# A two-layer decoder block pair in fp32: turned up-projections grouped by width, a second gate bank, sums of squares behind the last blocks, and a token factor moved to the output

## The chip, the cores and the metric

The kernel runs on one core of a Trainium2 chip. The metric is the device time of one launch in microseconds. TensorE is called PE in profile rows, its weight loads PEld, VectorE DVE, ScalarE ACT, GpSimd POOL and the queue of DMAs SP.

## What is computed

The input is one sequence of 256 tokens with 1024 features. A first network of two layers is followed by a second one of two layers. Cut to what the change touches:

```
first network, each layer:
    h = rms_norm(x, norm_mix);  proj = h @ w_in          # queries, keys, values, 2048 gate logits
    y_a = dilated_attention(...) @ w_proj_a
    y_b = stick_breaking_attention(...) @ w_proj_b
    gates = sigmoid(gate_logits + b_gate)
    x = x + (gates[:1024] * y_a + gates[1024:] * y_b) @ w_out
    h = rms_norm(x, norm_ffn)
    up = h @ w_up;  a, b = up[:2816], up[2816:]
    a = causal_conv(a, 3 taps) + conv_b
    x = x + (silu(a) * b) @ w_down
x = rms_norm(x, norm_final)
second network, each layer:
    x = x + rms_norm(mixer(rms_norm(x)));  x = x + rms_norm(cross_attention(rms_norm(x), mem))
    x = x + rms_norm(square(relu(rms_norm(x) @ w1)) @ w2)     # w1: 1024 x 4096
```

All matmuls are computed to nearly fp32 accuracy from operands split into a high and a low part: x @ w = xhi whi + xhi wlo + xlo whi.

## The kernel before

**Weights.** SP brings every weight matrix in chunks of 1 MB (2048 columns for each of 128 partitions) into three slots `raw`. Each chunk has two halves; ScalarE casts a half to `whi` (line 1416) and VectorE subtracts it to `wlo` (line 1799), into four slots; TensorE takes halves in one fixed order and waits on `lo_done`. All engines run through orders that are written out by hand, so where an engine waits, everything behind it on that engine waits too.

**Streams.** Ahead of a projection, `x` is turned on TensorE (line 960) in four blocks of 256 features. ScalarE writes the high part, scaled by the norm's gain (lines 1441 and 1442), and VectorE the low part (line 1826, two instructions a block, `stream_lo`). The first chunk behind a stream waits for block after block. The norm's factor per token, `rstd`, isn't in the stream: `squares` (line 1849, VectorE, two instructions of 1024 features) makes the sums, POOL the root (`root`, line 720), and the factor is applied to products later.

**Turned chunks** (`turned_half`, lines 870 to 891). The up-projections of the first network and w1 of the second yield feature rows instead of token rows: the weights are the stationary operand, the activations the moving one. For a block of 128 features (f = 0, 1) and each of 8 slices k of the inputs there is a wide matmul (line 888: `whi` times high and low part side by side, 512 columns) and a narrow one (line 889: `wlo` times the high part, 256 columns). So a chunk has 16 pairs, in two halves. There are 22 up blocks (11 in each layer) of two chunks each (a and b) and 32 chunks of w1 (16 in each layer). The first chunk behind a stream (four in all) is issued with that stream.

**Up-projection pipeline.** For each block: ScalarE copies the part that belongs to the low activations out of PSUM (lines 1582 and 1590), VectorE adds the other (lines 2111 and 2116), POOL multiplies a by the row of token factors (line 763), VectorE convolves (lines 2126 and 2132), ScalarE applies SiLU into `sl` (line 1604), POOL multiplies this by the row again into `gated` (line 768), VectorE multiplies by b (line 2146), and high and low part (lines 1610 and 2153) go into w_down, two blocks later. The row is made once for each layer: `spread_row`, two transposes on TensorE (line 902), and a copy by ScalarE (line 1498). At the end VectorE adds the product to x (line 2181).

**MLP pipeline.** ScalarE copies (1758), VectorE adds (2492), takes relu and multiplies by the row (2497), squares (2501), ScalarE makes the high part (1764) and VectorE the low one (2505). `spread_row` stands between w1(0) and w1(1) on TensorE.

**Gates.** The 2048 gate logits come in eight chunks of 256 columns, all accumulated in PSUM bank 7, both token tiles side by side. TensorE issues their halves between the steps of the attentions (`gate_half`): halves 2, 3 and 4 (chunk 1 and the first half of chunk 2) in a row, then the sums of the stick-breaking part, which wait for the four `keep` tiles of VectorE (line 2026); half 8 (chunk 4) stands behind the first scores of the dilated attention. VectorE evicts a chunk with the token factor and the bias (`gate_out`, line 1991, two instructions). Before chunk c starts, TensorE waits until chunk c-1 is out:

```
if h == 0 and c:
    pe.wait_ge(gate_pre, 2 * (NGC * l + c))
half_chunk(plan.jobs["gate", l, c][0], h, ahi, alo, 0, [[(0, GC, 7)], [(0, GC, 7)]], True, True, None, (0, GC))
```

## Time and profile before

| | |
|---|---|
| median of 3 runs | 1477.03 us (1476.95 to 1477.41) |
| the profiled execution | 1477.21 us, its span 1475.4 us |
| TensorE busy | 1418.3 us, 96% |
| VectorE busy | 1033.7 us, 70% |
| ScalarE busy | 735.8 us, 50% |
| POOL busy | 115.7 us, 8% |
| DMA | 242.36 MB, mean 164 GB/s |

Busy time of TensorE is modelled: a matmul's record goes on until its last column has left, while the next has long begun. Start-to-start distances tell its pace. "Idle before" is the time between the end of one record and the start of the next, so that a wait in start-to-start distance is some tenths of a microsecond longer than its idle time.

### The profile page before, as it was taken

How to read it: one execution, taken by the hardware profiler on the slowest of the kernel's cores; microseconds unless marked ns; L12 is line 12 of the kernel's file. 1: busy time of each engine (PE TensorE's matmuls, PEld its weight loads, DVE VectorE, ACT ScalarE, POOL GpSimd, SP SyncE). 2: the span in 40 equal slices, each digit the busy share in tenths (PEclk: the TensorE clock that was granted, in tenths of full speed). 3: DMA queues.
4: the chain of work that ended last, by engine and by line, in shares of the span. 5: the costliest groups of instructions: out<-in, count | busy, mean ns of one | idle time of the engine just before them, and what ended most of it. 6: DMA issues, size and time to landing. Idle time of an engine off the chain costs nothing.

```text
span 1475.4 us, 20204 instructions
## 1 busy us (share of the span) xinstructions
PE 1418.3 (96%) x7867; PEld 1187.4 (80%) x7867; DVE 1033.7 (70%) x1530; ACT 735.8 (50%) x1110; POOL 115.7 (8%) x115
## 2 busy tenths in 40 slices
PE   7999999999999999999999999999999999899997
PEld 5889888888788987888887777688888877688886
DVE  4565669888755557988887676786676757676665
ACT  4554445544455454544545554554444554544443
POOL 1000002111000000221212011000000000000000
PEclk9999999999999999999999999999999999999999
DMA  8743355555555326577656313258865504255562
GB/s 282 227 142 131 127 172 187 184 186 191 169 197 162 123 86 200 183 210 208 184 171 209 115 50 114 101 187 225 212 190 189 196 1 138 91 185 187 184 198 75
DMA packets 151618, 242.36 MB, mean 164 GB/s; under 512 B 4250, under 2 KB 102698, under 8 KB 151260
## 3 DMA queue, kind: packets, MB, share of 16 engines
q1 hardware_dynamic: 147780, 227.24, 47.8%
q0 software_dynamic: 3744, 13.84, 3.7%
q8 instruction: 63, 1.03, 0.3%
q14 instruction: 31, 0.25, 0.1%
HBM read 239.09 MB, written 1.97 MB: 163 GB/s over the span
## 4 chain that ended last, share of the span: by engine, by line
PE 88%; DVE 7%; ACT 2%; issue 1%; POOL 1%; DMA 1%; SPq 0%; DVEq 0%; ACTq 0%; POOLq 0%
PE ps L888 19%; PE ps L857 16%; PE ps L861 15%; PE ps L864 15%; PE ps L889 9%; PE ps L960 3%; PE ps L1035 2%; PE ps L1011 2%; PE ps L1026 1%; DVE wlo L1799 1%; PE ps L925 1%; DVE work L1849 1%; PE ps L927 1%; PE ps L926 1%; DVE act L1826 1%
## 5 line engine op out<-in xcount | busy, mean ns | idle before, releaser
L1799 DVE TENSOR_TENSOR wlo<-raw,whi 128x1024 fp32r<-128x1024 f32 (+1 forms) x436 | 560.0, 1296 | 195.4 <-ACT whi L1416 194.8
L1416 ACT CAST whi<-raw 128x1024 fp32r<-128x1024 f32 (+1 forms) x436 | 447.0, 1034 | 253.0 <-PE ps L864 168.8
L888 PE MATMUL ps<-act,whi 128*128 128x512 f32 x1216 | 433.3, 399 | 7.0 <-DVE act L1826 6.7
L889 PE MATMUL ps<-act,wlo 128*128 128x256 f32 x1216 | 341.3, 281 | 0.0
L888 PEld LDWEIGHTS ps<-act,whi 128*128 128x128 f32 x1216 | 228.4, 188 | 65.5 <-DVE act L1826 10.2
L889 PEld LDWEIGHTS ps<-act,wlo 128*128 128x128 f32 x1216 | 229.7, 189 | 1.7
L857 PE MATMUL ps<-whi,mhi 128*128 128x512 f32 (+2 forms) x656 | 220.0, 387 | 6.8 <-DVE mlo L1826 4.9
L861 PE MATMUL ps<-wlo,mhi 128*128 128x512 f32 (+2 forms) x656 | 215.3, 380 | 0.0
L864 PE MATMUL ps<-whi,mlo 128*128 128x512 f32 (+2 forms) x656 | 215.0, 379 | 0.0
L857 PE MATMUL ps<-whi,act 128*128 128x512 f32 (+1 forms) x544 | 190.7, 351 | 9.8 <-DVE region L1991 4.6
L864 PE MATMUL ps<-whi,act 128*128 128x512 f32 (+1 forms) x544 | 186.0, 342 | 0.0
L861 PE MATMUL ps<-wlo,act 128*128 128x512 f32 (+1 forms) x544 | 185.7, 341 | 0.0
L857 PEld LDWEIGHTS ps<-whi,mhi 128*128 128x128 f32 x656 | 119.8, 188 | 31.6 <-DVE mlo L1826 6.8
L864 PEld LDWEIGHTS ps<-whi,mlo 128*128 128x128 f32 x656 | 123.4, 188 | 24.2
L861 PEld LDWEIGHTS ps<-wlo,mhi 128*128 128x128 f32 x656 | 123.4, 188 | 23.6 <-issue 0.2
L857 PEld LDWEIGHTS ps<-whi,act 128*128 128x128 f32 x544 | 103.9, 191 | 26.0 <-DVE region L1991 5.4
L864 PEld LDWEIGHTS ps<-whi,act 128*128 128x128 f32 x544 | 103.7, 191 | 11.9
L861 PEld LDWEIGHTS ps<-wlo,act 128*128 128x128 f32 x544 | 104.0, 191 | 10.7
L1465 ACT ACTIVATE work<-work,low 128x256 f32<-128x256 f32 (+3 forms) x96 | 49.0, 511 | 71.2 <-DVE low L1866 70.2
L720 POOL TENSOR_TENSOR rstd<-ss,small 128x2 f32<-128x2 f32 x20 | 17.7, 883 | 753.8 <-DVE ss L2234 377.2
L1826 DVE SCALAR_TENSOR_TENSOR act<-ps,gains,act 128x256 fp32r<-128x256 f32 x64 | 27.3, 478 | 37.4 <-ACT act L1442 37.3
L1035 PE MATMUL ps<-proj,work 128*128 128x64 f32 (+1 forms) x336 | 44.1, 271 | 3.2 <-ACT work L1493 2.5
(231 smaller groups left out, 1440.1 us busy)
## 6 DMA issues: line engine op xcount, KB each, us to landing
raw<-in_mlp_w SPq DMA_DIRECT2D x64, 1024.0 KB, 5.3
raw<-in_w_up SPq DMA_DIRECT2D x44, 1024.0 KB, 5.2
raw<-in_w_in SPq DMA_DIRECT2D x40, 1024.0 KB, 5.2
raw<-in_w_down SPq DMA_DIRECT2D x22, 1024.0 KB, 4.8
raw<-in_ev_w_in SPq DMA_DIRECT2D x10, 1024.0 KB, 5.1
raw<-in_w_out SPq DMA_DIRECT2D x8, 1024.0 KB, 5.0
raw<-in_xa_wkv SPq DMA_DIRECT2D x4, 1024.0 KB, 5.1
raw<-in_ev_w_out SPq DMA_DIRECT2D x4, 1024.0 KB, 5.0
```

What stands on the lines that cost most here:

```text
L857: nc.tensor.matmul(o, hi[:, kx, rows_], wh[:, k, c0:c0 + w], start=first and h == 0 and k == 0 and (tt == 0 or at[1] == 0), stop=False)
L861: nc.tensor.matmul(o, hi[:, kx, rows_], wl[:, k, c0:c0 + w], start=False, stop=False)
L864: mm = nc.tensor.matmul(o, lo[:, kx, rows_], wh[:, k, c0:c0 + w], start=False, stop=final and h == 1 and k == kh - 1 and (tt == 1 or at[1] ...
L888: nc.tensor.matmul(both, wh[:, k, w], act2[:, kx].rearrange("p i n -> p (i n)"), start=kx == 0, stop=False)
L889: mm = nc.tensor.matmul(top, wl[:, k, w], act2[:, kx, 0], start=False, stop=kx == KD - 1)
L960: mm = nc.tensor.transpose(bank[:, j * P:j * P + P], src, ident)
L1011: m0 = nc.tensor.matmul(scores_of(*pair[0])[:, c0:c0 + n], q, k, start=True, stop=pair[0][1]["sel"] is None)
L1035: mm = nc.tensor.matmul(o, values_of(u, d)[:, b * P:b * P + P], v, start=b == 0, stop=b == len(d["pv"]) - 1)
L1416: nc.scalar.copy(whi[:, m % HL, 0:w], raw[:, n % RAW, h * w:h * w + w]).then_inc(hi_done, 1)
L1465: nc.scalar.activation(step_of(1536, u, d), step_of(0, u, d), ACT.Exp, scale=-1.0, bias=low[:, d["qt"], s:s + 1], accum_out=den[:, d["qt"] ...
L1799: nc.vector.tensor_tensor(wlo[:, m % HL, 0:w], raw[:, n % RAW, h * w:h * w + w], whi[:, m % HL, 0:w].bitcast(F32), ALU.subtract).then_inc( ...
L1826: ins = nc.vector.scalar_tensor_tensor(out=lo[:, 2 * g + b, :], in0=bank[:, b * SEQ:(b + 1) * SEQ], scalar=gains[:, 2 * g + b, row:row + 1 ...
```

## The change

1. In `turned_half` the matmuls of one f are issued as a group of wide ones and then a group of narrow ones: four and four in a half, two and two in the chunk that runs with a stream.
2. Gate chunks 1 and 3 go to the PSUM bank of 4 and 5 that the next turned group doesn't use; a chunk up to 4 waits for the eviction of the chunk before last, later ones for that of the last.
3. `squares` of the norms `xf` and `xm` stand behind the last stream block on VectorE; in the second network `spread_row` stands behind the second chunk of w1 on TensorE.
4. POOL's second multiplication (line 768) goes; VectorE multiplies b by `sl` directly. The factor per token is applied when the down-projection's product is added to x.

```diff
@@ turned_half
-                for k0 in range(0, kh, 2):
+                step = 2 if stream else kh
+                for k0 in range(0, kh, step):
                     if stream and k0:
                         stream["need"](place(2 * h + 1))
                     for f in range(2):
                         both, top = ps[:, bank0 + f, :], ps[:, bank0 + f, 0:SEQ]
-                        for k in (k0, k0 + 1):
+                        w = slice(f * P, f * P + P)
+                        for k in range(k0, k0 + step):
                             kx = kh * h + k
-                            w = slice(f * P, f * P + P)
                             nc.tensor.matmul(both, wh[:, k, w], act2[:, kx].rearrange("p i n -> p (i n)"), start=kx == 0, stop=False)
+                        for k in range(k0, k0 + step):
+                            kx = kh * h + k
                             mm = nc.tensor.matmul(top, wl[:, k, w], act2[:, kx, 0], start=False, stop=kx == KD - 1)
-                        if k0:
+                        if k0 + step == kh:
                             mm.then_inc(pe_out, 1)
@@ gates, TensorE and VectorE
+        def gate_bank(l, c):
+            return 9 - plan.groups["y1", l, "b"] % 2 - 4 if c in (1, 3) else 7
-                        pe.wait_ge(gate_pre, 2 * (NGC * l + c))
+                        pe.wait_ge(gate_pre, 2 * (NGC * l + (c if c > 4 else c - 1)))
-                    half_chunk(plan.jobs["gate", l, c][0], h, ahi, alo, 0, [[(0, GC, 7)], [(0, GC, 7)]], True, True, None, (0, GC))
+                    bank = gate_bank(l, c)
+                    half_chunk(plan.jobs["gate", l, c][0], h, ahi, alo, 0, [[(0, GC, bank)], [(0, GC, bank)]], True, True, None, (0, GC))
@@ POOL, the up-projection's block
-                    pool.wait_ge(silu_ready, g + 1)
-                    if g:
-                        pool.wait_ge(u_ready, g)
-                    nc.gpsimd.tensor_tensor(two(gated), two(sl), row, ALU.mult).then_inc(gate_scaled, 1)
@@ TensorE, second network
                 turned_chunk(plan.jobs["w1", l, 0][0], step_bank(0), stream("xm", l, x, x_half(x_count("yx", l)), spares=(13, 5, 7)))
+                turned_chunk(plan.jobs["w1", l, 1][0], step_bank(1))
                 spread_row("xm", l)
-                turned_chunk(plan.jobs["w1", l, 1][0], step_bank(1))
@@ ScalarE, ahead of SiLU
-                        act.wait_ge(gate_scaled, g)
+                        act.wait_ge(u_ready, g)
@@ VectorE, first network
-                stream_lo("xf", l, ahi, alo, row=gain_row["xf", l], gs=(2,))
+                stream_lo("xf", l, ahi, alo, row=gain_row["xf", l], gs=(2, 3))
                 squares(("xf", l), lambda tt: x[:, tt, :], D)
-                stream_lo("xf", l, ahi, alo, row=gain_row["xf", l], gs=(3,))
-                    dve.wait_ge(gate_scaled, g + 1)
+                    dve.wait_ge(silu_ready, g + 1)
-                    nc.vector.tensor_tensor(ut, up_b, gated, ALU.mult).then_inc(u_ready, 1)
+                    nc.vector.tensor_tensor(ut, up_b, sl, ALU.mult).then_inc(u_ready, 1)
-                        ins = nc.vector.tensor_tensor(xs, xs, ps[:, yb(tt, c), :], ALU.add)
+                        ins = nc.vector.scalar_tensor_tensor(out=xs, in0=ps[:, yb(tt, c), :], scalar=rstd[:, NORM["xf", l], tt:tt + 1],
+                                                             in1=xs, op0=ALU.mult, op1=ALU.add)
@@ VectorE, second network
                 split_half(n0 + 16)
-                squares(("xm", l), lambda tt: x[:, tt, :], D)
                 stream_lo("xm", l, ahi, alo, row=gain_row["xm", l], gs=(2,))
                 split_half(n0 + 17)
                 stream_lo("xm", l, ahi, alo, row=gain_row["xm", l], gs=(3,))
+                squares(("xm", l), lambda tt: x[:, tt, :], D)
                 split_half(n0 + 18)
```

What the change moves, at three places. **TensorE, end of the streamed chunk of w1 in layer 0 and what follows it** (L888 and L887 wide, L889 and L890 narrow, L902 and L903 the spread of the row). Before, between chunk w1(0) and w1(1):

```order
L888 MATMUL ps<-act,whi 128x512
L889 MATMUL ps<-act,wlo 128x256
L902 MATMUL ps<-cst,rstd 128x128 [waits rstd_ready]
L902 MATMUL ps<-cst,rstd 128x128
L888 MATMUL ps<-act,whi 128x512 [waits lo_done]
L889 MATMUL ps<-act,wlo 128x256
```

Now, the second half of w1(1), the spread, and the start of w1(2):

```order
L887 MATMUL ps<-act,whi 128x512 [waits lo_done]
L887 MATMUL ps<-act,whi 128x512 x3
L890 MATMUL ps<-act,wlo 128x256 x4
L887 MATMUL ps<-act,whi 128x512 x4
L890 MATMUL ps<-act,wlo 128x256 x4
L903 MATMUL ps<-cst,rstd 128x128 [waits rstd_ready]
L903 MATMUL ps<-cst,rstd 128x128
L887 MATMUL ps<-act,whi 128x512 [waits lo_done,m_sum]
```

Pairs have become groups of four, and the spread stands one chunk later.

**VectorE, the MLP's stream in layer 0** (L1826 and L1828 a stream block's low part, L1849 and L1851 the sums of squares, L1799 and L1801 a weight half's low part, L2497 and L2499 the multiply by the row). Before, from the weight half behind block 1 on:

```order
L1799 TENSOR_TENSOR wlo<-raw,whi 128x1024 [waits hi_done]
L1849 ISA work,ss<-x 128x1024 [waits ss_ready]
L1849 ISA ss 128x1
L1849 ISA work,ss<-x 128x1024 [waits ss_ready]
L1849 ISA ss 128x1
L1826 SCALAR_TENSOR_TENSOR act<-ps,gains,act 128x256 [waits grp_act]
L1826 SCALAR_TENSOR_TENSOR act<-ps,gains,act 128x256
L1799 TENSOR_TENSOR wlo<-raw,whi 128x1024 [waits hi_done]
L1826 SCALAR_TENSOR_TENSOR act<-ps,gains,act 128x256 [waits grp_act]
L1826 SCALAR_TENSOR_TENSOR act<-ps,gains,act 128x256
L1799 TENSOR_TENSOR wlo<-raw,whi 128x1024 [waits hi_done]
L2492 TENSOR_TENSOR work<-ps,work 128x512 [waits m_low]
```

Now, from the weight half ahead of block 3 on:

```order
L1801 TENSOR_TENSOR wlo<-raw,whi 128x1024 [waits hi_done]
L1828 SCALAR_TENSOR_TENSOR act<-ps,gains,act 128x256 [waits grp_act]
L1828 SCALAR_TENSOR_TENSOR act<-ps,gains,act 128x256
L1851 ISA work,ss<-x 128x1024 [waits ss_ready]
L1851 ISA ss 128x1
L1851 ISA work,ss<-x 128x1024 [waits ss_ready]
L1851 ISA ss 128x1
L1801 TENSOR_TENSOR wlo<-raw,whi 128x1024 [waits hi_done]
L2494 TENSOR_TENSOR work<-ps,work 128x512 [waits m_low]
L2499 SCALAR_TENSOR_TENSOR work<-work 128x512 [waits m_sum,row_ready]
L2503 TENSOR_TENSOR work<-work 128x512 [waits chain]
L1801 TENSOR_TENSOR wlo<-raw,whi 128x1024 [waits hi_done] x2
```

The sums stand behind block 3, between it and the next weight half; behind the multiply that waits for the row stand two weight halves.

**VectorE, the up-projection's stream in layer 0**, from block 2 on. Before:

```order
L1826 SCALAR_TENSOR_TENSOR act<-ps,gains,act 128x256 [waits grp_act,x_ready]
L1826 SCALAR_TENSOR_TENSOR act<-ps,gains,act 128x256
L1849 ISA work,ss<-x 128x1024 [waits ss_ready]
L1849 ISA ss 128x1
L1849 ISA work,ss<-x 128x1024 [waits ss_ready]
L1849 ISA ss 128x1
L1826 SCALAR_TENSOR_TENSOR act<-ps,gains,act 128x256 [waits grp_act]
L1826 SCALAR_TENSOR_TENSOR act<-ps,gains,act 128x256
L1799 TENSOR_TENSOR wlo<-raw,whi 128x1024 [waits hi_done]
```

Now:

```order
L1828 SCALAR_TENSOR_TENSOR act<-ps,gains,act 128x256 [waits grp_act,x_ready]
L1828 SCALAR_TENSOR_TENSOR act<-ps,gains,act 128x256
L1828 SCALAR_TENSOR_TENSOR act<-ps,gains,act 128x256 [waits grp_act]
L1828 SCALAR_TENSOR_TENSOR act<-ps,gains,act 128x256
L1851 ISA work,ss<-x 128x1024 [waits ss_ready]
L1851 ISA ss 128x1
L1851 ISA work,ss<-x 128x1024 [waits ss_ready]
L1851 ISA ss 128x1
L1801 TENSOR_TENSOR wlo<-raw,whi 128x1024 [waits hi_done]
```

Block 3 follows block 2 directly, the sums come behind both.

## Rows read from the trace of the kernel before

**Rows 1.** the page: span; busy us (share) xinstructions

```profile
span 1475.4 us, 20204 instructions
...
PE 1418.3 (96%) x7867; PEld 1187.4 (80%) x7867; DVE 1033.7 (70%) x1530; ACT 735.8 (50%) x1110; POOL 115.7 (8%) x115
```

**Rows 2.** costliest groups: line engine op, out<-in | busy us, mean ns

```profile
L888 PE MATMUL ps<-act,whi 128*128 128x512 f32 x1216 | 433.3, 399 | 7.0 <-DVE act L1826 6.7
...
L889 PEld LDWEIGHTS ps<-act,wlo 128*128 128x128 f32 x1216 | 229.7, 189 | 1.7
```

**Rows 3.** timeline of TensorE, MLP: start us, duration us, what, [idle before <-releaser]

```profile
968.30 0.40 PE L888 MATMUL ps<-act,whi 128*128 128x512 f32 x1
...
978.70 0.39 PE L888 MATMUL ps<-act,whi 128*128 128x512 f32 x1
...
1001.28 0.63 PE L857 MATMUL ps<-whi,mhi 128*128 128x512 f32 x2
...
1006.29 0.61 PE L864 MATMUL ps<-whi,mlo 128*128 128x512 f32 x2
...
1007.09 0.40 PE L888 MATMUL ps<-act,whi 128*128 128x512 f32 x1
...
1011.68 0.40 PE L888 MATMUL ps<-act,whi 128*128 128x512 f32 x1
```

**Rows 4.** timeline of TensorE in the gate chunks of layer 0

```profile
98.80 0.28 PE L861 MATMUL ps<-wlo,act 128*128 128x256 f32 x1
...
102.16 0.28 PE L864 MATMUL ps<-whi,act 128*128 128x256 f32 x1
103.41 0.39 PE L857 MATMUL ps<-whi,act 128*128 128x256 f32 x1 [0.97 <-DVE region L1991]
...
122.46 0.27 PE L1012 MATMUL ps<-qT 64*128 64x128 f32 x1
124.06 0.39 PE L857 MATMUL ps<-whi,act 128*128 128x256 f32 x1 [1.33 <-DVE region L1991]
```

**Rows 5.** timeline of VectorE, the four keep tiles

```profile
103.27 1.96 DVE L2026 SCALAR_TENSOR_TENSOR work<-work 128x384 f32<-128x384 f32 x4
```

**Rows 6.** waits over the span: who <- whom: us in total, times, longest

```profile
PE ps L888 <- DVE act L1826: 6.7, 8, 1.5
...
PE ps L857 <- DVE region L1991: 4.6, 4, 1.3
```

**Rows 7.** timeline at the up-projection's stream in layer 0, three engines

```profile
207.00 0.47 ACT L1442 ACTIVATE act<-ps,gains 128x256 fp32r<-128x256 f32 x1
...
209.01 0.87 DVE L1826 SCALAR_TENSOR_TENSOR act<-ps,gains,act 128x256 fp32r<-128x256 f32 x2
...
209.93 0.50 PE L888 MATMUL ps<-act,whi 128*128 128x512 f32 x1 [1.52 <-DVE act L1826]
```

**Rows 8.** timeline at the MLP's stream in layer 0, three engines

```profile
962.05 1.05 ACT L1416 CAST whi<-raw 128x1024 fp32r<-128x1024 f32 x1
...
960.98 1.22 DVE L1849 CUSTOM_DVE_ANT_0 work<-x 128x1024 f32<-128x1024 f32 x1
...
969.35 0.69 DVE L2497 SCALAR_TENSOR_TENSOR work<-work 128x512 f32<-128x512 f32 x1
...
970.69 1.22 DVE L1799 TENSOR_TENSOR wlo<-raw,whi 128x1024 fp32r<-128x1024 f32 x1
...
964.32 0.50 PE L888 MATMUL ps<-act,whi 128*128 128x512 f32 x1 [1.18 <-DVE act L1826]
...
966.23 0.50 PE L888 MATMUL ps<-act,whi 128*128 128x512 f32 x1 [0.24 <-DVE act L1826]
```

**Rows 9.** busy us of PE, PEld, DVE, ACT, POOL in up-projections

```profile
220.00:385.00 165.00, 165.00 (x866) 140.58 (x865) 143.67 (x167) 85.29 (x102) 30.49 (x21) 1.00 0.57 185
```

**Rows 10.** groups by form, as in rows 2, of two VectorE lines

```profile
L2223 DVE SCALAR_TENSOR_TENSOR x<-work,rstd,x 128x512 f32<-128x512 f32 x24 | 16.5, 747 | 1.2 <-POOL rstd L720 1.2
...
L2181 DVE TENSOR_TENSOR x<-x,ps 128x512 f32<-128x512 f32 x8 | 5.3, 685 | 1.5 <-PE ps L927 1.5
```

More of the change, by code:

```diff
@@ L314, in build_network @@
         rstd_row = work[:, 1536:1536 + SEQ]
-        gated = work[:, 3584:4096]
         low_part = work[:, 4096:4608]
@@ L404, in build_network @@
         silu_ready = sem("silu_ready")
-        gate_scaled = sem("gate_scaled")
         u_ready = sem("u_ready")
@@ L1990, in gate_out @@
                         dve.wait_ge(pe_out, 4 * plan.jobs["gate", l, c][0] + 4)
-                        nc.vector.scalar_tensor_tensor(out=gates[:, tt, at], in0=ps[:, 7, GC * tt:GC * (tt + 1)],
+                        nc.vector.scalar_tensor_tensor(out=gates[:, tt, at], in0=ps[:, gate_bank(l, c), GC * tt:GC * (tt + 1)],
                                                        scalar=rstd[:, NORM["x1", l], tt:tt + 1], in1=gate_bias[:, at],
```

## The prediction, made before the changed kernel ran

> **What bounds the kernel now.** I read the page first. TensorE is busy for 96% of the span [rows 1], so this kernel ends when TensorE has issued its matmuls; what can be won is matmul time or a stretch in which TensorE sits idle. VectorE comes second, and I keep it in view as the engine that could take over. The groups by cost then name what the change touches: 1216 wide matmuls at line 888, each followed by a narrow one at line 889, every one with a weight load of its own that is recorded at 189 ns [rows 2]. A matmul's recorded duration overlaps the next, so what counts is the distance from start to start, and that is read in the timeline. In the MLP, from 1007.09 to 1011.68 us, there are 13 pairs of wide and narrow: 4.59/13 = 0.353 us for a pair [rows 3]. In the down-projection just ahead of it, where all matmuls are wide, 22 of them start in 5.01 us (1001.28 to 1006.29): 0.2277 us each [rows 3]. In the gate chunks, where all are narrow (256 columns), 28 start in 3.36 us (98.80 to 102.16): 0.120 us each [rows 4]. So a wide and a narrow one would take 0.347 us if each ran among its own kind, and take 0.353 us when they alternate. The last view is the waits: TensorE sits idle four times for the eviction of a gate chunk (4.6 us) and eight times for the low part of a stream block in front of line 888 (6.7 us) [rows 6]. The change aims at these three places.
>
> **1. Matmuls grouped by width.** Nothing is added or removed, only ordered. There are 1216/16 = 76 turned chunks of 16 pairs: 22 up blocks of 2 chunks and 32 MLP chunks. Four of them are streamed (groups of two), 72 are not (groups of four wide, then four narrow). A pair loses 353.0 - (227.7 + 120.0) = 5.3 ns, or 6 to 7 ns if the wide one is put at its shortest, 226.7; I take 6.5. Before, every pair pays; in groups of four one round in four does, so a pair gains 4.9 ns: 72 x 16 x 4.9 ns = 5.6 us. The streamed ones, with one round in two, gain 64 x 3.3 ns = 0.2 us. Together **-5.8 us**. Bounds: if the loss isn't in the switch of width at all, 0; if groups lose nothing at their borders, 1216 x 6.5 ns = 7.9 us. The trace has no run that goes four and four, so I take the price by the number of switches, which lies between.
>
> **2. The second gate bank.** Chunk c of the gates waits until chunk c-1 has been evicted from bank 7. In layer 0 this costs 103.41 - 102.16 - 0.12 = 1.13 us ahead of chunk 2, and 124.06 - 122.46 - 0.20 = 1.40 us ahead of chunk 4 [rows 4]; layer 1 has the same two waits (four in all [rows 6]). In the new order chunks 1 and 3 lie in another bank, chunk 2 waits only for chunk 0, and chunk 4 only for chunk 2, both of which were evicted long before. What is late next? Behind the first half of chunk 2 TensorE takes the four keep tiles of the stick-breaking part, one every 0.9 us, from 105.3 us in the new order; VectorE makes them from 103.27 to 105.23, the first by 103.8 [rows 5], so they are in time, if only just. In the dilated attention behind the second wait the timeline shows no idle time of TensorE. So I take all of it: 2 x 2.53 = **-5.1 us**. Bounds: nothing more is to be had here; if the keep tiles held TensorE up instead, 2 x 1.40 = 2.8 us would remain.
>
> **3. Sums of squares behind the last block, up-projection.** TensorE waits at 209.93 us, idle for 1.52 us, for the low part of the last block; VectorE makes the sums of squares first and starts this low part, 0.87 us long, at 209.01. ScalarE has the high part ready at 207.00 + 0.47 = 207.47 [rows 7]. Now the low part comes right behind that: 207.52 + 0.87 = 208.39, and TensorE starts at 208.44, that is 1.49 us earlier, x 2 layers = **-3.0 us**. The sums end some 0.9 us later than they did (at 210.9 instead of 209.0 plus the low part), which is hidden: POOL's root and the row are needed only behind two whole chunks (2 x 5.6 us).
>
> **4. The same in the MLP, and the row moved behind the second chunk.** Here VectorE does a low part of a weight chunk, the squares (two of 1.22 us from 960.98), block 2, a weight chunk, block 3; TensorE waits for block 2 until 964.32 and for block 3 until 966.23 [rows 8]. Without the squares block 2 starts when ScalarE's high part is ready (its next instruction starts at 962.05), so at about 962.2, and ends at 963.1; the weight chunk, cast by 963.10, is subtracted by 964.3; block 3 is ready at 965.2: 1.0 us earlier. But the spread of the row now sits behind chunk w1(1) on TensorE: 965.2 + 1.5 (four pairs) + 5.6 = 972.3, and no longer behind the four pairs of block 3. ScalarE copies the row (0.38 us), and until then it is not free for the next weight chunk; VectorE is stopped at its multiply by the row, which starts at about 973.1 instead of 969.35, and behind it on its queue stand the square and the low part of the weights for the second half of w1(2). From the multiply to that subtraction it is 970.69 - 969.35 = 1.34 us, and the subtraction takes 1.22 [rows 8]: 973.1 + 1.34 + 1.22 = 975.7. TensorE wants that half at 972.4 + 2.9 = 975.3. So a **new wait of about 0.4 us** takes the place of part of the old one, and perhaps 0.1 more in the next chunk. Net 1.0 - 0.5 = 0.5 us, x 2 = **-1.0 us** (between -2.1 if VectorE keeps up, and +0.5 if the new wait is three times what I think).
>
> **5. The token factor moved to the output.** POOL loses 22 multiplications and VectorE takes the SiLU directly. In the up-projections TensorE has no idle time (165.00 of 165.00 us busy) while POOL is busy for 30.49 us and VectorE for 143.67 [rows 9], so this is worth **0** by itself; it gives VectorE slack, and should that slack not be needed nobody sees it. On the way out, eight additions become multiply-adds with a factor per token: 685 ns for the one kind, 747 ns for the other [rows 10], so 62 ns each; only the last one or two before a stage border are waited for: **+0.1 us** in all (0 to 0.5).
>
> **The sum.** -5.8 - 5.1 - 3.0 - 1.0 + 0.1 = -14.8 us. The profiled execution took 1477.21 us (span 1475.4), so 1462.4; the median of the runs shown is 1477.03, 0.18 lower, so I forecast **1462.2 us**. A measurement of this kernel can tell about 0.2% (3 us) from no change.
>
> **Rivals.**
> A. *The alternation costs nothing, something else does.* Two chunks in the MLP alternate all the same and run at (978.70 - 968.30)/30 = 0.3467 us a pair [rows 3], so the 6 ns may belong to how the engines happen to stand to each other and not to the switch. Then term 1 is 0: 1468.0 us. Against it: the other 70 unstreamed chunks run at 0.353. Chance 0.15.
> B. *The stalls only move.* Where TensorE comes earlier, the chain of ScalarE and VectorE behind it is late instead: half of terms 2 to 4 (9.1 us) comes back as waits for the masks, for the first attention scores and for the weights. Then 1477.0 - 5.8 - 4.5 = 1466.7 us. For it: term 4 shows one such wait; against it: in the attention and in the up-projections TensorE shows no idle time now, and all that it waits for there is made from its own results, so it moves with it. Chance 0.13.
> C. *Narrow matmuls in a row are bound by their weight loads; slower.* Alternating, two loads have 353 ns in which to hide. Four narrow ones in a row leave a load only the 120 ns of its predecessor. If the recorded 189 ns of a load [rows 2] were its real pitch, three of four narrow ones would take 189 instead of 120 ns: 72 x 12 x 69 ns = 60 us more, and with terms 2 to 5 the time would be 1477.0 + 60 - 9 = 1528 us. It decides as soon as a load takes longer than the 120 ns from start to start; to cancel the other gains it needs 10 ns. The gate chunks speak against it: they load a block for each narrow matmul and keep 0.120 us [rows 4]. Chance 0.02.
> The Trainium skill, "TensorE: Matmul & The Clock Gate" (Part 3, what overlaps and what doesn't), states that a weight load overlaps matmuls in flight only where the row group differs. By that rule the loads here, which all use the full array, would not hide, and C would hold; the gate rows at 0.120 us, shorter than one load, do not bear the rule out for this kernel.
> D. *No change that can be measured*, since what is won is lost to something that I don't see: 1477 us, chance 0.03. The rest, 0.67, is the forecast.
>
> **Range and chances.** From the forecast 1462.2 down to where groups lose nothing at their borders (-2.1) and the MLP has no new wait (-1.1), 1459.0; up to A at 1468.0 with a little for B on top: 1468.5. That leaves out C, D and the far end of A with B together, less than 2 in 10. Faster by more than 3 us: the forecast, A, B: 0.95. Within: 0.03. Slower: 0.02.
>
> **What the profile afterwards would show.** Term 1: four wide starts 0.227 apart, then four narrow ones 0.120 apart, and a chunk of 16 pairs in about 5.57 us instead of 5.65; wrong if the narrow ones stand 0.13 or more apart, or if the chunk still takes 5.65. Term 2: no row of TensorE waiting for the gate eviction. Term 3: the wait near 209 us gone but for 0.2 us. Term 4: block 3 ready 1 us earlier, and a new idle time of 0.3 to 0.5 us in front of the second half of w1(2), ended by the low half of the weights. Term 5: POOL at half its instructions in the up-projections, no change of TensorE there. The prediction is wrong as a whole if TensorE shows new waits of more than 3 us in sum, or if the pair's pitch doesn't fall.

## The result, and the profile after

| | before | after |
|---|---|---|
| median of 6 runs each, same chip | 1477.22 us (1476.80 to 1480.01) | 1465.13 us (1464.40 to 1467.37) |
| ratio | | 0.9918, 95% interval 0.9905 to 0.9931 |
| span of the profiled execution | 1475.4 us | 1463.6 us |

The changed kernel is faster by 12.1 us (10 to 14 by the interval); 1462.2 had been forecast, and 1465.13 lies inside the range of 1459.0 to 1468.5. In the changed kernel the wide matmuls are line 887, the narrow ones 890, the spread of the row 903; the low half of the weights is line 1801, the low part of a stream block 1828, the sums of squares 1851, POOL's root 722.

The page, in the columns of [rows 1, 2], with VectorE's largest group and POOL's root:

```profile
span 1463.6 us, 20161 instructions
...
PE 1415.2 (97%) x7867; PEld 1187.6 (81%) x7867; DVE 1012.6 (69%) x1530; ACT 737.2 (50%) x1110; POOL 87.3 (6%) x93
...
L1801 DVE TENSOR_TENSOR wlo<-raw,whi 128x1024 fp32r<-128x1024 f32 (+1 forms) x436 | 539.5, 1249 | 203.4 <-ACT whi L1418 202.6
...
L887 PE MATMUL ps<-act,whi 128*128 128x512 f32 x1216 | 335.6, 395 | 2.5 <-DVE act L1828 1.9
...
L722 POOL TENSOR_TENSOR rstd<-ss,small 128x2 f32<-128x2 f32 x20 | 21.3, 1065 | 774.8 <-DVE ss L1851 377.5
```

Line 887's 335.6 us against the 433.3 of [rows 2] isn't time won: busy time counts overlapping records once, and wide ones now overlap each other. The idle time ahead of them is 2.5 us instead of 7.0. Of the waits, in the columns of [rows 6], the one for the gate eviction is gone, the one for the low part of the stream fell from 6.7 to 1.9 us, and one is new:

```profile
PE ps L887 <- DVE act L1828: 1.9, 6, 0.4
...
PE ps L887 <- DVE wlo L1801: 0.5, 2, 0.3
```

Where the 11.8 us of span come from is read from the start of the same matmul in both timelines (the first wide one of a turned block; in the MLPs, of stream block 1):

| stretch of TensorE | before | after | difference |
|---|---|---|---|
| start of the kernel to the first up-projection | 202.73 | 200.75 | -1.98 |
| up-projections, layer 0, first block to last | 160.22 | 157.73 | -2.49 |
| last block of layer 0 to the first of layer 1 (gates of layer 1) | 214.38 | 211.61 | -2.77 |
| up-projections, layer 1 | 160.18 | 157.73 | -2.45 |
| to the MLP, layer 0 | 223.53 | 222.93 | -0.60 |
| MLP, layer 0 | 156.77 | 156.02 | -0.75 |
| to the MLP, layer 1 | 169.55 | 169.43 | -0.12 |
| MLP, layer 1 | 157.01 | 156.41 | -0.60 |
| the rest | 31.03 | 30.99 | -0.04 |

The first row holds a loss too: the wait for the very first DMA took 8.1 instead of 7.3 us in this execution, so the gates of layer 0 gave some 2.7 us. And 0.37 us of the row "to the MLP, layer 0" isn't the change's: it is a wait in the second network's first mixer that was shorter in this execution (1.16 us instead of 1.53), and that changes from trace to trace, as shown below. The up-projections and the gates gave what was forecast or nearly; the two MLPs gave 1.35 us where terms 1 and 4 had promised about 3.5.

**The pace.** Timeline of TensorE in the MLP, columns as in [rows 3] (a row's x4 are four matmuls in succession), two blocks:

```profile
1040.33 1.07 PE L887 MATMUL ps<-act,whi 128*128 128x512 f32 x4
1041.23 0.64 PE L890 MATMUL ps<-act,wlo 128*128 128x256 f32 x4
1041.71 1.09 PE L887 MATMUL ps<-act,whi 128*128 128x512 f32 x4
1042.64 0.63 PE L890 MATMUL ps<-act,wlo 128*128 128x256 f32 x4
1043.11 1.09 PE L887 MATMUL ps<-act,whi 128*128 128x512 f32 x4
...
1051.40 1.07 PE L887 MATMUL ps<-act,whi 128*128 128x512 f32 x4
```

The first group behind the down-projection takes 1041.71 - 1040.33 = 1.38 us for four pairs (345 ns a pair), the next 1.40 (350 ns). Four wide ones start 0.90 us apart in the first group, 0.93 in the others: in a group of four, 0.227 each is reached only behind other wide ones. A block (16 pairs and the down-projection's step) takes 1051.40 - 1040.33 = 11.07 us; before it was 11.107 (first wide ones at 1017.85 and 1028.96). In the up-projections a block of 32 pairs fell from 16.793 to 16.687 us.

**The gates.** Timeline of TensorE around chunk 1 and 2 of layer 0; the waits of [rows 4] are gone, and the sums that need the keep tiles start right behind:

```profile
102.09 0.28 PE L862 MATMUL ps<-whi,act 128*128 128x256 f32 x1
102.21 0.28 PE L855 MATMUL ps<-whi,act 128*128 128x256 f32 x1
102.33 0.28 PE L859 MATMUL ps<-wlo,act 128*128 128x256 f32 x1
...
105.69 0.28 PE L862 MATMUL ps<-whi,act 128*128 128x256 f32 x1
105.81 0.38 PE L1141 MATMUL ps<-work,cst 128*128 128x128 f32 x2
```

**The MLP's stream in layer 0**, all engines, columns as in [rows 8]:

```profile
952.84 0.73 PE L887 MATMUL ps<-act,whi 128*128 128x512 f32 x2
...
954.91 0.72 PE L887 MATMUL ps<-act,whi 128*128 128x512 f32 x2 [0.40 <-DVE act L1828]
...
957.18 1.22 DVE L1801 TENSOR_TENSOR wlo<-raw,whi 128x1024 fp32r<-128x1024 f32 x1
...
957.35 1.62 POOL L722 TENSOR_TENSOR rstd<-ss,small 128x2 f32<-128x2 f32 x1 [8.87 <-DVE ss L1851]
...
962.00 0.38 PE L903 MATMUL ps<-cst,rstd 128*128 128x128 f32 x2
...
962.41 0.37 ACT L1500 COPY work<-ps 128x256 f32<-128x256 f32 x1 [5.23 <-PE ps L903]
...
962.82 0.69 DVE L2499 SCALAR_TENSOR_TENSOR work<-work 128x512 f32<-128x512 f32 x1 [3.82 <-ACT work L1500]
...
964.15 1.22 DVE L1801 TENSOR_TENSOR wlo<-raw,whi 128x1024 fp32r<-128x1024 f32 x1
...
965.42 1.19 PE L887 MATMUL ps<-act,whi 128*128 128x512 f32 x4 [0.25 <-DVE wlo L1801]
```

Block 2 (952.84) no longer waits, block 3 still does, 0.40 us. From the spread at 962.00 the chain runs as forecast: copy, multiply (VectorE idle for 3.82 us ahead of it), square, low half of the weights from 964.15 to 965.37, and TensorE, which would have been due at 965.02, starts at 965.42.

### The profile page after: what moved, and what is told of

It is laid out like the page before. It is cut to its first block, busy times and chain, and to the rows that moved or that the text cites. A ratio compares the mean times of both kernels' runs of the same rounds, so it can differ in the third digit from the quotient of the medians.

```text
span 1463.6 us, 20161 instructions
## 1 busy us (share of the span) xinstructions
PE 1415.2 (97%) x7867; PEld 1187.6 (81%) x7867; DVE 1012.6 (69%) x1530; ACT 737.2 (50%) x1110; POOL 87.3 (6%) x93
## 4 chain that ended last, share of the span: by engine, by line
PE 88%; DVE 6%; ACT 2%; issue 1%; POOL 1%; DMA 1%; SPq 0%; DVEq 0%; ACTq 0%; POOLq 0%
PE ps L887 18%; PE ps L855 16%; PE ps L862 15%; PE ps L859 15%; PE ps L890 9%; PE ps L961 3%; PE ps L1036 2%; PE ps L1012 2%; PE ps L1027 1%; DVE wlo L1801 1%; PE ps L926 1%; PE ps L928 1%; PE ps L927 1%; ACT whi L1418 1%; DVE x L2225 1%
## 5 line engine op out<-in xcount | busy, mean ns | idle before, releaser
L1801 DVE TENSOR_TENSOR wlo<-raw,whi 128x1024 fp32r<-128x1024 f32 (+1 forms) x436 | 539.5, 1249 | 203.4 <-ACT whi L1418 202.6
L887 PE MATMUL ps<-act,whi 128*128 128x512 f32 x1216 | 335.6, 395 | 2.5 <-DVE act L1828 1.9
L887 PEld LDWEIGHTS ps<-act,whi 128*128 128x128 f32 x1216 | 209.6, 189 | 35.0 <-DVE act L1828 4.6
L890 PEld LDWEIGHTS ps<-act,wlo 128*128 128x128 f32 x1216 | 188.6, 189 | 27.1
L890 PE MATMUL ps<-act,wlo 128*128 128x256 f32 x1216 | 195.7, 281 | 0.0
L855 PEld LDWEIGHTS ps<-whi,mhi 128*128 128x128 f32 x656 | 119.7, 188 | 29.7 <-DVE mlo L1828 6.4
L862 PEld LDWEIGHTS ps<-whi,act 128*128 128x128 f32 x544 | 103.7, 191 | 11.8
L722 POOL TENSOR_TENSOR rstd<-ss,small 128x2 f32<-128x2 f32 x20 | 21.3, 1065 | 774.8 <-DVE ss L1851 377.5
L1828 DVE SCALAR_TENSOR_TENSOR act<-ps,gains,act 128x256 fp32r<-128x256 f32 x64 | 27.3, 478 | 42.8 <-ACT act L1444 42.7
L765 POOL TENSOR_TENSOR work<-work 128x512 f32<-128x512 f32 x22 | 33.3, 1516 | 272.8 <-DVE work L2112 265.1
```

The costliest lines, as they stand in the source:

```text
L765: nc.gpsimd.tensor_tensor(two(up_as), two(up_a), row, ALU.mult).then_inc(a_scaled, 1)
L855: nc.tensor.matmul(o, hi[:, kx, rows_], wh[:, k, c0:c0 + w], start=first and h == 0 and k == 0 and (tt == 0 or at[1] == 0), stop=False)
L862: mm = nc.tensor.matmul(o, lo[:, kx, rows_], wh[:, k, c0:c0 + w], start=False, stop=final and h == 1 and k == kh - 1 and (tt == 1 or at[1] ...
L887: nc.tensor.matmul(both, wh[:, k, w], act2[:, kx].rearrange("p i n -> p (i n)"), start=kx == 0, stop=False)
L890: mm = nc.tensor.matmul(top, wl[:, k, w], act2[:, kx, 0], start=False, stop=kx == KD - 1)
L1801: nc.vector.tensor_tensor(wlo[:, m % HL, 0:w], raw[:, n % RAW, h * w:h * w + w], whi[:, m % HL, 0:w].bitcast(F32), ALU.subtract).then_inc( ...
```

## Experiments

The four kernels with one part each ran on one chip; two_two, eight_eight, spread_half and spread_early on a second; two_cross, four_cross, two_and_spread and after_again on a third. Each set shares the runs of the kernel before on its chip. Six of these kernels ran only once; what is said of them rests on their timelines.

### One part alone, four times

**only_group**: the kernel before with `turned_half` of the changed one.

```diff
-                        for k in (k0, k0 + 1):
-                            (wide, narrow)
+                        for k in range(k0, k0 + step):
+                            (wide)
+                        for k in range(k0, k0 + step):
+                            (narrow)
```

> The kernel before with part 1 alone (four wide, four narrow). Theory S (a price per switch of width, 6.5 ns a pair, as predicted): 1477.2 - 5.8 = 1471.4 us, a pair at 348.2 ns. Theory R (narrow matmuls put TensorE into a slower pace of some 7 ns a matmul, out of which it comes only after about a dozen wide ones in a row): a pair at 350.3 ns as in the changed kernel, an MLP block at 11.073 us instead of 11.107, an up block at 16.687 instead of 16.793, together 22 x 0.107 + 32 x 0.033 = 3.4 us: 1473.8 us.

Measured: 1474.27 us against 1477.98, ratio 0.9977 (0.9966 to 0.9987); block times 16.687 and 11.073 us, as in the changed kernel. So the grouping alone gives 3.7 us (2 to 5), and it gives the same with everything else left as it was. The price for each switch of width that term 1 assumed doesn't hold.

**only_gates**: the kernel before with the second bank.

```diff
-                        pe.wait_ge(gate_pre, 2 * (NGC * l + c))
+                        pe.wait_ge(gate_pre, 2 * (NGC * l + (c if c > 4 else c - 1)))
# and bank = gate_bank(l, c) in place of 7, on TensorE and VectorE
```

> The kernel before with part 2 alone (second gate bank). Predicted 5.1 us less; the changed kernel's trace shows 2.7 us a layer, so 5.4: 1471.8 us. Rival (the stalls only move): 1474.5. Four waits of TensorE for line 1991 become none.

Measured: 1472.59 us, ratio 0.9965 (0.9952 to 0.9977). TensorE has no wait for the eviction, and the stretch from the last up block of layer 0 to the first of layer 1 fell from 214.38 to 211.75 us: 2.63 us a layer, against 2.53 in the working.

**only_squares**: the kernel before with `squares` behind the last blocks and the spread behind the second chunk of w1.

```diff
# the second network, VectorE; squares of xf and the spread of the row move as in the change
-                squares(("xm", l), lambda tt: x[:, tt, :], D)
                 stream_lo("xm", l, ahi, alo, row=gain_row["xm", l], gs=(2,))
                 split_half(n0 + 17)
                 stream_lo("xm", l, ahi, alo, row=gain_row["xm", l], gs=(3,))
+                squares(("xm", l), lambda tt: x[:, tt, :], D)
```

> The kernel before with part 3 and 4 alone (sums of squares behind the last blocks, the row behind the second chunk). Predicted -3.0 in the up-projections and -1.0 in the MLP: 1473.2 us. Rival for the MLP: the new wait for the weight half eats the whole gain there: 1474.2 or more. In the trace: an idle time of TensorE of 0.25 us or more in the second half of w1(2), ended by the low half of the weights.

Measured: 1473.07 us, ratio 0.997 (0.9957 to 0.9983). From the third stream block of the up-projections to the spread of the row TensorE takes 9.00 us instead of 10.50 in layer 0 (term 3: 1.49). In the MLP TensorE now waits at the new place even with the old pace:

```profile
PE ps L888 <- DVE act L1826: 1.6, 4, 0.4
```

That is what is left of the 6.7 us of [rows 6]; in front of the second half of w1(2) it idles for 0.23 us in each layer, released by the low half of the weights (line 1799).

**only_factor**: the kernel before without POOL's second multiplication, with the factor at the output.

```diff
-                    nc.gpsimd.tensor_tensor(two(gated), two(sl), row, ALU.mult).then_inc(gate_scaled, 1)
-                        ins = nc.vector.tensor_tensor(xs, xs, ps[:, yb(tt, c), :], ALU.add)
+                        ins = nc.vector.scalar_tensor_tensor(out=xs, in0=ps[:, yb(tt, c), :], scalar=rstd[:, NORM["xf", l], tt:tt + 1],
+                                                             in1=xs, op0=ALU.mult, op1=ALU.add)
```

> The kernel before with part 5 alone (POOL's second multiplication gone, factor in the final add). Predicted 0 to +0.3 us: 1477.3 us. Rival: POOL's instruction slowed VectorE enough to hold TensorE up somewhere, then up to 1 us less. VectorE's busy time falls by some 20 us in any case, since its subtraction takes 2.3 us instead of 1.2 where it meets a POOL multiplication.

Measured: 1477.26 us, ratio 0.9999 (0.9988 to 1.0011): nothing, though the page shows 20 us less of VectorE and 30 less of POOL:

```profile
PE 1417.3 (96%) x7867; PEld 1186.7 (80%) x7867; DVE 1013.5 (69%) x1530; ACT 737.1 (50%) x1110; POOL 85.5 (6%) x93
```

The four medians add up to -3.7 - 5.4 - 4.9 - 0.7 = -14.7 us; by their ratios -0.23 - 0.35 - 0.30 - 0.01 = -0.89% or -13.1 us, against -12.1 for the whole. Within the intervals the parts add.

### How long should a group be?

Three kernels change only the order inside a half of the changed one: **two_two** (two wide, two narrow everywhere), **eight_eight** (all eight wide ones of both f, then all eight narrow ones), and the changed kernel's four and four between them.

```diff
# two_two
-                step = 2 if stream else kh
+                step = 2
# eight_eight, for each half
                     for f in range(2):
                         (wide ones)
+                    for f in range(2):
                         (narrow ones)
```

> The changed kernel with groups of two wide and two narrow in every turned chunk. Theory S (price per switch): the pair lies half-way between alternation and no switch, 350 ns; that is no worse than the groups of four measured (350.3). Theory R (slower pace after narrow ones, left only after many wide ones): two wide ones never leave it, so 353 ns as in the alternation, an MLP block at 11.107 us.

> The changed kernel with eight wide and then eight narrow ones in a half (both feature blocks). Theory S: 347.5 ns a pair. Theory R: the eight wide ones leave the slower pace after five to ten, the narrow ones stay at 119 to 120; about 349 ns a pair, an MLP block at 11.05 us, an up block at 16.64.

Measured, one execution each: 1460.88 and 1463.18 us (the kernel before beside them: 1479.05). The timeline gives the pace without scatter: in every execution the blocks agree to 1 or 2 ns, those next to a stream left out.

| order | switches of width in a half | up block | MLP block | a pair, by the up block |
|---|---|---|---|---|
| one and one (before) | 15 | 16.793 us | 11.107 us | as it was |
| two and two | 7 | 16.587 | 11.013 | -6.4 ns |
| four and four (the change) | 3 | 16.687 | 11.073 | -3.3 ns |
| eight and eight | 1 | 16.614 | 11.027 | -5.6 ns |

(The last column is the difference of the up block over 32 pairs; the MLP block over its 16 gives -5.9, -2.1 and -5.0 ns, in the same order.) Both theories fell: with fewer switches it does not get steadily faster, and two and two, which should have been the worst of the three, is the best. Timeline of TensorE in two_two, one block of the MLP:

```profile
1047.96 0.62 PE L887 MATMUL ps<-act,whi 128*128 128x512 f32 x2
1048.41 0.40 PE L890 MATMUL ps<-act,wlo 128*128 128x256 f32 x2
1048.64 0.63 PE L887 MATMUL ps<-act,whi 128*128 128x512 f32 x2
1049.11 0.39 PE L890 MATMUL ps<-act,wlo 128*128 128x256 f32 x2
1049.34 0.62 PE L887 MATMUL ps<-act,whi 128*128 128x512 f32 x2
...
1053.52 0.62 PE L855 MATMUL ps<-whi,mhi 128*128 128x512 f32 x2
...
1058.97 0.62 PE L887 MATMUL ps<-act,whi 128*128 128x512 f32 x2
```

Four pairs take 1049.34 - 1047.96 = 1.38 us; a steady round of two pairs takes 0.696 us. The single starts, in ns to the next, are 233, 236 (wide), 116, 112 (narrow), 232, 231, 114, 119 and again: the wide ones stay slow, at 233 instead of 227, but the narrow ones stand at 115 instead of 120. In the changed kernel a round of four is 234, 236, 228, 232 and 118, 119, 118, 116, then 235, 234, 235, 225 and 117, 120, 120, 120. In eight and eight a round is 233, 236, 228, 233, 231, 226, 227, 228 and 113 and then seven at 119 to 121.

**two_cross** and **four_cross** ask whether it is the PSUM bank: they keep the number of switches but alternate the two f inside a group, so that no two neighbours (two_cross) or only half of them (four_cross) write into one bank.

```diff
# two_cross (four_cross: for k in (k1, k1 + 1) inside each f)
+                    for k in (k0, k0 + 1):
+                        for f in range(2):
+                            (wide of f, k)
+                        for f in range(2):
+                            (narrow of f, k)
```

> The changed kernel, with the wide and the narrow matmuls of both features blocks interleaved by two: for each slice k wide f0, wide f1, narrow f0, narrow f1. There are as many switches of width as with two wide and two narrow of one f (a pair at 348.3 ns, up block 16.587 us, MLP block 11.013 us, 1460.9 us), but neighbours never write to the same PSUM bank. Theory 'length of the group alone': the same pace, an up block of 16.58 to 16.61 us, an MLP block of 11.01 us, 1461 us (within 1). Theory 'a bank kept for all four matmuls is what makes the groups of two cheap': the pair falls back to the alternating 353.3 ns, an up block of 16.79 us, an MLP block of 11.11 us, 1461 + 206 x 0.022 = 1465.5 us or more.

> The changed kernel, with groups of four that span both feature blocks: wide f0 k, f0 k+1, f1 k, f1 k+1, then the four narrow ones in the same order. As many switches of width as in the changed kernel (a pair at 350.3 ns, up block 16.687 us, MLP block 11.073 us, 1463.6 us span), but a bank changes in the middle of each group. Theory 'length of the group alone': the pace of the changed kernel, 16.69 and 11.07 us, device time 1465 us within 1.5. Theory 'the bank matters': another pace; if staying in one bank for two matmuls is what is cheap, 16.59 and 11.01 us as with groups of two, 1461 us.

Measured, one execution each: 1460.54 us, blocks 16.587 and 11.013; and 1464.63 us, blocks 16.687 and 11.073. Both to the last digit what the same length of group gave in one bank. Timeline of two_cross, one block:

```profile
1047.63 0.62 PE L886 MATMUL ps<-act,whi 128*128 128x512 f32 x2
...
1058.64 0.61 PE L886 MATMUL ps<-act,whi 128*128 128x512 f32 x2
```

So in groups of two and four the pace goes with the length of the group, not with the bank and not with which sum a matmul continues. What in TensorE or in the loading of its weights makes it so was not found.

### Where should the row be spread?

**spread_half** is the changed kernel with the spread between the two halves of w1(1); **spread_early** has it before w1(1), where it stood before the change.

```diff
# spread_half
-                turned_chunk(plan.jobs["w1", l, 1][0], step_bank(1))
-                spread_row("xm", l)
+                turned_chunk(plan.jobs["w1", l, 1][0], step_bank(1), between=lambda: spread_row("xm", l))
# spread_early
+                spread_row("xm", l)
                 turned_chunk(plan.jobs["w1", l, 1][0], step_bank(1))
-                spread_row("xm", l)
```

> The changed kernel with the spread of the row between the two halves of w1(1) instead of behind the chunk. The root is ready 0.7 us behind the sums of squares, which end about 2.5 us behind block 3, so TensorE has it when the first half is over. If the late row causes the new waits of TensorE in w1(2) and behind, they vanish and the MLP's start is 0.4 us (layer 0) and 0.7 us (layer 1) shorter. Rival: the squares themselves, which now stand ahead of the weight half on VectorE, cause them: then they stay.

> The changed kernel with the spread of the row back in front of w1(1), but the sums of squares behind the last block. TensorE reaches it 1.5 us behind block 3, while the sums take 2.4 us and the root 0.7: it waits 1.5 to 1.7 us at the spread in each layer, more than the wait that the change has.

spread_half, one execution: 1467.37 us in all, which settles nothing (below); but in its timeline the waits for the low half of the weights are gone in both layers, and from block 1 of the stream to chunk w1(3) TensorE takes 22.55 us instead of 23.12 and 23.16, with the next block at 11.07 instead of 11.45 in layer 1. That is 0.6 and 1.0 us, 1.6 for both layers, as expected: the new wait is an effect of where the spread stands.

spread_early, one execution: 1472.12 us. TensorE, POOL and VectorE in layer 0:

```profile
958.68 1.22 DVE L1801 TENSOR_TENSOR wlo<-raw,whi 128x1024 fp32r<-128x1024 f32 x1
958.85 1.62 POOL L722 TENSOR_TENSOR rstd<-ss,small 128x2 f32<-128x2 f32 x1 [8.88 <-DVE ss L1851]
...
960.53 0.69 PE L903 MATMUL ps<-cst,rstd 128*128 128x128 f32 x2 [2.46 <-POOL rstd L722]
960.87 2.05 PE L887 MATMUL ps<-act,whi 128*128 128x512 f32 x4
```

The wait is 2.46 us, not the 1.5 to 1.7 expected, because the root took 1.62 us instead of 0.71. So moving the spread was a necessary part of the change: with the squares last and the spread at its old place, the MLP's stream would have lost more than it won: in layer 1, at full clock, block 1 of the stream to w1(3) takes 25.22 us here, 23.73 in the kernel before and 23.16 in the changed one. It also cost TensorE its clock. Stretches of the same execution: busy us of PE, PEld, DVE, ACT and POOL, then the granted clock as a share of 2.4 GHz, layer 0 and then layer 1:

```profile
960.00:961.00 1.00, 0.47 (x3) 0.47 (x3) 0.50 (x1) 0.00 (x0) 1.00 (x2) 0.55 0.16 50
961.00:962.00 1.00, 1.00 (x5) 0.81 (x4) 0.34 (x1) 0.75 (x2) 0.20 (x1) 0.50 0.45 33
962.00:963.00 1.00, 1.00 (x5) 0.81 (x4) 0.97 (x3) 0.57 (x1) 0.00 (x0) 0.50 0.61 131
963.00:964.00 1.00, 1.00 (x6) 0.94 (x6) 1.00 (x2) 0.62 (x1) 0.00 (x0) 0.74 1.02 422
...
1289.00:1290.00 1.00, 0.54 (x4) 0.50 (x5) 0.43 (x1) 0.07 (x1) 0.41 (x1) 1.00 0.14 44
```

From just before the end of the wait in layer 0, the clock was granted at 0.50, that is 1.2 GHz, for some 3.4 us ((0.45 + 0.50 + 0.50 + 0.26)/0.50), and the four wide matmuls from 960.87 took 2.05 us instead of 1.1; behind the same wait (2.47 us) in layer 1 it stayed at 1.00.

### The version that beats both

**two_and_spread** joins two_two and spread_half; **after_again** is the changed kernel, run beside it on the same chip.

```diff
-                step = 2 if stream else kh
+                step = 2
-                turned_chunk(plan.jobs["w1", l, 1][0], step_bank(1))
-                spread_row("xm", l)
+                turned_chunk(plan.jobs["w1", l, 1][0], step_bank(1), between=lambda: spread_row("xm", l))
```

> The version meant to beat both: groups of two wide and two narrow everywhere (up block 16.587 instead of 16.687 us, MLP block 11.013 instead of 11.073 us), and the spread of the row in the MLP between the two halves of w1(1), where VectorE gets it early enough for the second half of w1(2). If the two gains add: 22 x 0.10 + 32 x 0.06 = 4.1 us from the groups and 0.6 + 1.0 = 1.6 us from the spread, 5.7 us below the changed kernel, 1459.4 us (1458 to 1461). If the spread's gain is already contained in the groups' (TensorE then comes earlier and waits longer for VectorE), 1461 us and an idle time of 0.2 us ahead of the second half of w1(2) is still there.

> The changed kernel unaltered, so that it stands beside the version meant to beat it on the same chip and in the same rounds: 1464 to 1466 us, 12 us below the kernel before; up block 16.687 us and MLP block 11.073 us if the pace of a group of four belongs to the code and not to one execution; within 0.03 us a block otherwise.

Measured: two_and_spread 1461.27 us (1458.84 to 1462.45), ratio to the kernel before 0.9888 (0.9874 to 0.9903); after_again 1466.39 us (1463.63 to 1469.02), ratio 0.9924 (0.9911 to 0.9937). The slowest run of the one is faster than the fastest of the other, and the difference of the medians, 5.1 us, is close to the 5.7 expected. In the timeline both gains are there: blocks of 16.587 and 11.013 us, and 22.50 us for that stretch of the MLP's start, with no wait for the low half of the weights. The four stretches of up-projections and MLPs are 4.9 us shorter in sum than in the table of the result. From the times alone the two gains couldn't be told apart, since after_again itself scatters by 5 us.

Where this scatter comes from shows in its trace. The same stretches of the changed kernel in the profiled execution of the result, and in that of after_again, columns as above:

```profile
780.00:790.00 10.00, 8.84 (x39) 6.98 (x38) 7.06 (x11) 4.77 (x7) 4.01 (x3) 1.00 0.65 216
1200.00:1210.00 10.00, 8.33 (x58) 6.74 (x57) 5.29 (x12) 5.69 (x13) 0.00 (x0) 1.00 0.01 2
```

```profile
780.00:790.00 10.00, 8.09 (x29) 6.15 (x28) 7.06 (x11) 4.66 (x7) 4.02 (x3) 0.83 0.59 198
1200.00:1210.00 10.00, 8.61 (x59) 7.21 (x56) 4.98 (x16) 3.92 (x14) 0.00 (x0) 0.85 0.01 2
```

In each of the two places TensorE stands at half its clock for some 3 us (0.17 x 10/0.5 = 3.4), which costs about 1.7 us; the span was 1467.2 us instead of 1463.6. Both lie in the second network. The second stands behind a wait of 0.97 us that is as long in the other execution, and the stretch it lies in (last block of the MLP of layer 0 to the MLP of layer 1) is 1.6 us longer. The first stands behind a wait that is itself longer, 1.91 us instead of 1.16, and its stretch is 2.4 us longer: 1.7 for the clock, 0.75 for the wait. The wait is TensorE's, ScalarE and a DMA are its source. ScalarE casts a weight half ahead of the high part of the stream, and waits for the weights of the mixer to land; first the execution of the result, then after_again:

```profile
778.40 1.06 ACT L1418 CAST whi<-raw 128x1024 fp32r<-128x1024 f32 x1 [1.92 <-DMA raw<-in_ev_w_in]
782.71 0.50 PE L855 MATMUL ps<-whi,mhi 128*128 128x512 f32 x1 [1.16 <-DVE mlo L1828]
```

```profile
778.70 1.05 ACT L1418 CAST whi<-raw 128x1024 fp32r<-128x1024 f32 x1 [2.69 <-DMA raw<-in_ev_w_in]
783.00 0.50 PE L855 MATMUL ps<-whi,mhi 128*128 128x512 f32 x1 [1.91 <-DVE mlo L1828]
```

In the fourteen traces TensorE's wait here runs from 0.24 to 2.31 us, and wherever ScalarE's wait can be read TensorE's is 0.8 us shorter. VectorE adds to it: one of the two sums of squares, 1.22 us, stands directly ahead of the low part that TensorE waits for, as it did in the streams that the change reordered; whether moving it helps was not tried. The half clock stands behind it in the four traces with the longest waits (1.86, 1.91, 2.18 and 2.31 us). The last two are spread_early and spread_half: this place takes 2.9 us more in spread_half than in the execution of the result, which explains its 1467.37. So a single time of these kernels says little by itself; the length of one block does.

## Why the prediction was right, and where it failed

**As a whole**: faster by more than 3 us, as given with a chance of 0.95; the time 2.9 us above the forecast, in the range. That it stayed in the range is owed to the bounds of term 1, not to its price.

**Term 1, the grouping (-5.8): the term that failed.** The step that failed is "I take the price by the number of switches". The pair's loss of 5 to 6.5 ns against pure runs was read rightly, and the bounds (0 and 7.9) held, but it isn't shared out by switches: four and four wins 3.3 ns a pair instead of 4.9 in the up-projections and (11.107 - 11.073)/16 = 2.1 in the MLP, in all 22 x 0.106 + 32 x 0.034 = 3.4 us instead of 5.8; only_group measured 3.7. With two and two, to which the same step gave 3.3 ns, a pair wins 6.4. Of the sign "four wide starts 0.227 apart, then four narrow ones 0.120 apart" the first half held only for the first group behind a down-projection: behind narrow ones a wide group stands 0.233 apart. The row that would have warned was there and was used for rival A only: alternating chunks that ran at 0.3467 [rows 3]. An alternating sequence had two paces, so the pace could not be a sum of prices for switches.

**Term 2, the gates (-5.1)**: 2.63 to 2.7 us a layer, -5.3. The keep tiles were in time: VectorE made them from 103.92, and TensorE began with them at 105.81 without idle time.

**Term 3, squares in the up-projections (-3.0)**: 1.50 us in layer 0 by only_squares. Right, but for a side reading: the sums do not end 0.9 us later than before. POOL's root starts at 208.88 instead of 209.17 in a stretch that begins 1.98 us earlier, so they end 1.7 us later, and it is hidden all the same.

**Term 4, the MLP's stream (-1.0)**: mechanism and place right, size too high. The new wait was forecast at 0.4 us and is 0.40 from start to start, before the very half that was named (as idle time 0.25, a little under the 0.3 to 0.5 that the sign gave); but in layer 1 a second one follows (the next block takes 11.447 instead of 11.073), and before the change w1(1) and w1(2) of layer 0 had run at the faster of the two alternating paces, which the grouping took away. From block 1 of the stream to w1(3) it gave 0.38 us in layer 0 and 0.57 in layer 1, less 0.37 there: -0.6 in all, the grouping of three chunks included. Without the grouping, in only_squares, these stretches and the block behind them gave 0.5 us in all, half of what was forecast.

**Term 5, the token factor (+0.1)**: nothing to be measured, 0.9999. It did give VectorE 20 us of slack, and TensorE needed none of it.

**The difference**: 5.8 - 3.4 = 2.4 us are term 1's, about 0.5 term 4's, less 0.2 that the gates gave more; the rest lies within the scatter of the runs. In the profiled execution the wait for the first DMA was 0.8 us longer and the one in the first mixer 0.37 us shorter; neither is the change's.

**The rivals.** A, grouping worth nothing: excluded, only_group's interval ends at 0.9987. B, the stalls only move: false for the gates and the squares of the up-projections (both waits gone, the stretches shorter by as much), true in small for the MLP. C, narrow ones bound by their loads: false; four narrow ones stand 0.113 to 0.120 apart under loads recorded at 189 ns. By the rule of the Trainium skill that had been set beside C, "TensorE: Matmul & The Clock Gate" (Part 3, what overlaps and what doesn't), they would not have hidden; the changed kernel's rows contradict it as those of the gates did.

## What to carry to other kernels

Take a stall out by the second buffer or by putting what nobody waits for behind what is waited for, and walk on along the queue behind the moved work: here the forecast of the next wait was right to 0.1 us, and putting the spread half a chunk earlier removed that one too. But don't extrapolate the pace of back-to-back matmuls from pure runs and a price per switch: run two or three group lengths, read the start-to-start distance of one block (it repeats to 1 ns, when the whole time scatters by 2 to 5 us), and keep the best. An engine's busy time that falls is worth nothing where it wasn't waited for.

## What the runs showed of the hardware

- **The pace of alternating matmuls depends on the sequence, and not steadily.** A pair of 512 and 256 columns, each with its own load, takes 353, 348, 350 and 349 ns in groups of one, two, four and eight; the bank has no part in it. Groups of one had a second pace of 347 ns in some stretches [rows 3], which the code doesn't choose: with the same order of matmuls the stretch behind the first up-projection's stream (four chunks and one step of the down-projection) takes 28.16 us in the kernel before and 27.74 in only_factor. In starts, the slow alternation is 236, 114, 232, 118, 240, 120 ns and again, three pairs long; the fast one is 230 and 117. The cause is open.
- **A wide run behind narrow ones is slow at first.** Behind a narrow group the down-projection's first starts stand 235, 233, 236, 224, 231, 236, 228, 233 and 231 ns apart before they come to 227.
- **POOL's small root takes 1.62 us instead of 0.71 beside VectorE's subtraction.** Before, the low part of a stream block (one input from PSUM) ran beside it; now a subtraction with both inputs in SBUF does (957.18 to 958.40, the root 957.35 to 958.97). It works the other way too: in the up-projections of the changed kernel a subtraction that meets POOL's multiplication took 2.19 us instead of 1.23.

```profile
265.53 1.29 POOL L765 TENSOR_TENSOR work<-work 128x512 f32<-128x512 f32 x1 [15.40 <-DVE work L2112]
265.71 2.19 DVE L1801 TENSOR_TENSOR wlo<-raw,whi 128x1024 fp32r<-128x1024 f32 x1 [0.26 <-ACT whi L1418]
268.09 1.23 DVE L1801 TENSOR_TENSOR wlo<-raw,whi 128x1024 fp32r<-128x1024 f32 x1 [0.19 <-ACT whi L1418]
```

  The Trainium skill, "SBUF — State Buffer" ("Who interferes with whom"), says that a VectorE instruction with two SBUF inputs and a GpSimd instruction that reads SBUF take turns at a shared read port, whoever comes first holding it for its whole length. These rows agree: what the later one loses, 0.91 and 0.96 us, is about what was left of the first (1.05 and 1.11 us). Fewer POOL multiplications to meet also explain why line 1801 has a mean of 1249 ns, where the kernel before had 1296 in its page: in only_factor, which takes POOL's second multiplication out and nothing else of POOL, the same subtraction has 1248, and in the three kernels that keep it (only_group, only_gates, only_squares) 1297.
- **TensorE's clock falls behind some waits, and not behind the same wait elsewhere.** Behind 2.46 us in one layer it was granted at 0.50 for some 3.4 us, behind 2.47 us in the other it stayed at 1.00; and the same code had or had not such a stretch from one execution to the next, at about 1.7 us each. Eight of the fourteen traces have one near 30 us too, the two of the result among them (29.7 to 33.1 us in the kernel before).
